# One stage for a layer's three attentions, and a row maximum ahead of the coefficients in attention B

## What is computed

```
s = einsum(q, k) * 64 ** -0.5;  p = softmax(s)
a = p[:, :, 0] - lam * p[:, :, 1]
o = einsum(a, v)
```

## Time and profile before

| | |
|---|---|
| median of 3 runs | 5782.29 us (5776.59 to 5786.37) |
| the profiled execution, its own time | 5787.31 us |
| its span | 5785.7 us |
| busy share: PE, PE weight loads, DVE, ACT, POOL | 84%, 72%, 53%, 45%, 20% |
| mean granted TensorE clock | 0.919 of full speed |
| the six attention stages, first PE instruction to last DVE output | 679 to 1012 (A), 1041 to 1295 (B), 1313 to 1493 (C); layer 1: A ends 3895, B 3923 to 4140, C 4157 to 4312 |

### The profile page before, as it was taken

One profiled execution on the slowest core, in us unless ns is written; L12 is line 12 of the kernel. 1 busy time (PEld: TensorE's weight loads), 2 busy tenths in 40 slices (PEclk: granted clock), 3 DMA queues, 4 the chain that ended last, 5 costly groups with the idle time before them and its releaser, 6 DMA issues. The chain is left out here.

```text
span 5785.7 us, 81996 instructions
## 1 busy us (share of the span) xinstructions
PE 4841.5 (84%) x28941; PEld 4176.1 (72%) x28941; DVE 3075.4 (53%) x4748; ACT 2589.9 (45%) x3394; POOL 1180.8 (20%) x1097
## 2 busy tenths in 40 slices
PE   5688899688798877799982788998889897599995
PEld 0688889678686776688762788987787686487774
DVE  1555155566433444677756551546563433577775
ACT  0344245456422331677762342545552221377773
POOL 0344200450000000333333340005300000233333
PEclk7799999899899988899996999998999998799997
DMA  8433441415333354799986432224353325599997
GB/s 370 168 94 96 180 146 39 100 50 125 127 120 135 139 204 169 285 397 397 397 324 226 152 95 85 62 50 109 76 142 117 144 106 190 192 397 397 397 397 288
DMA packets 596310, 1111.39 MB, mean 192 GB/s; under 512 B 112400, under 2 KB 295984, under 8 KB 589456
## 3 DMA queue, kind: packets, MB, share of 16 engines
q1 hardware_dynamic: 550576, 956.42, 48.1%
q0 software_dynamic: 29504, 94.50, 4.2%
q10 hardware_dynamic: 16032, 57.88, 2.5%
HBM read 908.23 MB, written 200.45 MB: 192 GB/s over the span
## 5 line engine op out<-in xcount | busy, mean ns | idle before, releaser
L643 PE MATMUL project_proj_acc<-project_w_split,project_hT 128*128 128x256 f32 x5472 | 727.7, 293 | 0.0
L643 PEld LDWEIGHTS project_proj_acc<-project_w_split,project_hT 128*128 128x128 f32 x5472 | 697.1, 200 | 0.3 <-issue 0.2
L1455 PE MATMUL merge_acc<-merge_hT,merge_w_split 128*128 128x512 f32 (+1 forms) x2880 | 634.1, 376 | 20.6 <-issue 16.9
L1455 PEld LDWEIGHTS merge_acc<-merge_hT,merge_w_split 128*128 128x128 f32 x2880 | 508.3, 191 | 129.6 <-issue 22.1
L2062 DVE TENSOR_TENSOR experts_w_gate<-experts_raw_gate,experts_w_gate 128x2048 fp32r<-128x2048 f32 x148 | 368.7, 2498 | 362.2 <-ACT experts_w_gate L2014 362.1
L1999 POOL TENSOR_TENSOR experts_w_down<-experts_raw_down,experts_w_down 128x2048 fp32r<-128x2048 f32 x74 | 361.4, 4883 | 536.9 <-ACT experts_w_down L2014 536.9
L2109 PE MATMUL experts_gate_acc<-experts_w_gate,experts_rowsT 128*128 128x512 f32 x1776 | 437.3, 402 | 13.8 <-DVE experts_rowsT L2067 10.1
L2123 PE MATMUL experts_result_acc<-experts_w_down,experts_hiddenT 128*128 128x512 f32 x1776 | 436.5, 401 | 12.2 <-DVE experts_w_down L2062 12.2
L2109 PE MATMUL experts_up_acc<-experts_w_up,experts_rowsT 128*128 128x512 f32 x1776 | 426.4, 395 | 0.0
L2109 PEld LDWEIGHTS experts_gate_acc<-experts_w_gate,experts_rowsT 128*128 128x128 f32 x1776 | 332.3, 190 | 101.6 <-issue 18.4
L2014 ACT CAST experts_w_gate<-experts_raw_gate 128x2048 fp32r<-128x2048 f32 x148 | 282.4, 1913 | 269.3 <-DMA experts_raw_gate<-in_w_exp_gate_dram 197.5
(11 more groups left out here) (220 smaller groups left out, 8506.6 us busy)
## 6 DMA issues: line engine op xcount, KB each, us to landing
experts_raw_gate<-in_w_exp_gate_dram SPq DMA_DIRECT2D x148, 1024.0 KB, 13.9
experts_raw_up<-in_w_exp_up_dram SPq DMA_DIRECT2D x148, 1024.0 KB, 12.9
experts_raw_down<-in_w_exp_down_dram SPq DMA_DIRECT2D x148, 1024.0 KB
merge_w_raw<-in_w_merge_dram SPq DMA_DIRECT2D x120, 768.0 KB, 6.6
modulation_w_ada<-in_w_ada_dram SPq DMA_DIRECT2D x48, 1024.0 KB, 27.1
qk<-project_staged SPq DMA_DIRECT2D x168, 256.0 KB, 2.3
ye<-experts_result ACTq DMA_DIRECT2D x74, 512.0 KB, 6.3
ye<-attend_a_zeros POOLq DMA_DIRECT2D x52, 512.0 KB, 27.4
```

Of the source, the lines that this page charges most:

```text
L643: m = pe.matmul(acc[s % 4][:, 0:HALF], hT[:, a, k, t * P:(t + 1) * P], w_split[hf][:, c, k, :], start=(i == 0 and k == 0), stop=(i == 2 an ...
L1455: m = pe.matmul(acc[:, bank, 0:w], w_split[b][:, a, k0 + k, :], act_T[:, x, kk, 0:w], start=(i == 0 and k == 0), stop=(i == 2 and k == n - 1))
```

## The change

Four edits:

1. The three attention stages become one, stage_attend. stage_attend_gqa and stage_attend_b turn into functions that return their parts per engine. Each engine runs A's, B's and C's part one after another, without a barrier between. A and C share their SBUF buffers, all three share the unit matrix and the PSUM buffers. B has its own SBUF buffers. SP issues A's first loads, then B's first loads (the four lambda vectors, head 0, and head 1 without its queries), then A's loop, then C's first loads, B's loop, C's loop, and then waits for all outputs. C's first loads wait for A's last scores and values. PE starts B when A's last output is ready (A's yd), and C when B's is.
2. In B, DVE takes the row maximum of set 0 of step s ahead of the coefficients of step s-1.
3. In project, the first table alone is made before POOL's loop, and needs only the rotary table and the first gain. The other five are made in group 0, one after each of POOL's steps 2 to 6. DVE waits for 3 table instructions in front of its first L555, and for all 18 at the end of group 0.
4. In output_and_route, the second activation tile is loaded between the w_out rows (after k = 5), the unit matrix and router weights come before the modulation rows, and PE waits for them after the products of tile 1 instead of after those of tile 0.

```diff
@@ project_heads
             for n, kind in enumerate(KINDS):
-                sp.dma_start(gain[:, n, :], io[kind][l].partition_broadcast(P)).then_inc(tab_in.sem, 16)
+                sp.dma_start(gain[:, n, :], io[kind][l].partition_broadcast(P)
+                             ).then_inc((more_in if n else tab_in).sem, 16)
...
                     if isinstance(g, int) and g == 0:
-                        dve.wait_ge(tab.sem, tab.done(6 * 3 - 1))
+                        dve.wait_ge(tab.sem, tab.done(3 - 1))
...
+                if isinstance(p, int) and p == 0:
+                    dve.wait_ge(tab.sem, tab.done(6 * 3 - 1))
...
                     if exists(q):
                         rest_of_heads(q, r)
+                    if isinstance(p, int) and p == 0 and s in range(2, 2 + 5):
+                        if s == 2:
+                            pool.wait_ge(more_in.sem, more_in.done(4))
+                        make_table(s - 1)
+                if isinstance(p, int) and p == 0:
+                    pool.wait_ge(tab.sem, tab.done(6 * 3 - 1))
+            pool.wait_ge(tab_in.sem, tab_in.done(1))
+            make_table(0)
+            pool.wait_ge(tab.sem, tab.done(3 - 1))
             pairs(pool, body)
@@ attend_gqa, SP: the first load of C
+            if isinstance(i, int) and i == 0 and first:
+                sp.wait_ge(first.qk.sem, first.qk.done(4 * NS - 1))
+                sp.wait_ge(first.pv.sem, first.pv.done(4 * NS - 1))
@@ attend_gqa, PE
+        if banded:
+            pe.wait_ge(const_split.sem, const_split.done(1))
+            pe.wait_ge(before_it.yd.sem, before_it.yd.done(before_it.last))
+        else:
+            pe.wait_ge(const_in.sem, const_in.done(0))
@@ attend_b, SP
+    def sync_first(sp):
+        load_kv, load_q, _ = loads(sp)
+        y_out.credit(sp)
+        for j, name in enumerate(("lambda_q1", "lambda_q2", "lambda_k1", "lambda_k2")):
+            sp.dma_start(lam_in[:, j, :], io[name][l].partition_broadcast(P)).then_inc(lam_ld.sem, 16)
+        load_kv(0, 0, None)
+        load_q(0, 0)
+        load_q(0, 1)
+        load_kv(1, 1, None)
@@ attend_b, DVE
             for s in range(nq):
+                row_max(n, s, 0)
                 q, r = before(n, s - 1)
                 if exists(q):
                     coefficients(q, r)
-                row_max(n, s, 0)
                 row_max(n, s, 1)
@@ stage_attend
+                sp.dma_start(shared.ident[:, :], io["k_ident"]).then_inc(shared.const_in.sem, 16)
+                a.sync_first(sp)
+                b.sync_first(sp)
+                a.sync(sp)
+                c.sync_first(sp)
+                b.sync(sp)
+                c.sync(sp)
+                for part in (a, b, c):
+                    part.sync_last(sp)
...
+            def _(pe):
+                for part in (a, b, c):
+                    part.tensor(pe)
@@ output_and_route, SP
                 sp.dma_start(w_raw[k % RAW][:, :], io["w_out"][l, k * P:(k + 1) * P, :]).then_inc(w_in[k % RAW].sem, 16)
-                if k == 1:
-                    load(0, 0)
+                if k in (1, 5):
+                    load(0, k // 5)
+            sp.dma_start(ident[:, :], io["k_ident"]).then_inc(const_in.sem, 16)
+            sp.dma_start(wr[:, :, :], io["w_router"][l]).then_inc(const_in.sem, 16)
             mod_rows(scr, l, 2, gate[:, :, :], sp).then_inc(rows_in.sem, 16)
             mod_rows(scr, l, 3, shift[:, :, :], sp).then_inc(rows_in.sem, 16)
             mod_rows(scr, l, 4, scale[:, :, :], sp).then_inc(rows_in.sem, 16)
-            load(0, 1)
-            sp.dma_start(ident[:, :], io["k_ident"]).then_inc(const_in.sem, 16)
-            sp.dma_start(wr[:, :, :], io["w_router"][l]).then_inc(const_in.sem, 16)
@@ output_and_route, PE
                         first_output()
-                        pe.wait_ge(const_in.sem, const_in.done(1))
                     else:
                         output(p, b)
+                    if isinstance(t, int) and t == 1:
+                        pe.wait_ge(const_in.sem, const_in.done(1))
```

More of the change, by code:

```diff
@@ new lines, in attend_gqa, with by_dve, wait_copied, before @@
+    steps = [Step(s % nq, banded) for s in range(NS)]
+    n_dve = sum(sx.n > sx.by_act for sx in steps)
+    def by_dve(i, s):
+        if steps[s].n > steps[s].by_act:
+            return i * n_dve + sum(sx.n > sx.by_act for sx in steps[:s])
+    def wait_copied(eng, i, s):
+        if exists(i):
+            eng.wait_ge(ca.sem, ca.done(i * NS + s))
+            if by_dve(i, s) is not None:
+                eng.wait_ge(cv.sem, cv.done(by_dve(i, s)))
+    def before(i, s):
+        return (i, s) if s >= 0 else (i - 1, s + NS)
@@ new lines, in attend_b, with before @@
+    lm, cf, df, tr, ca, pv, rc, yd = (
+        st.event("lambda_step"), st.event("coefficient_step"), st.event("b_difference"),
+        st.event("b_probs_transposed"), st.event("b_copied_out"), st.event("b_values_summed"),
+        st.event("b_reciprocal"), st.event("b_out_ready"))
+    dd, p1_scaled = st.event("difference_by_dve"), st.event("p1_scaled")
+    taken = st.event("pool_waits_taken")
+    steps = [Step(t, False) for t in range(nq)]
+    def before(n, s):
+        return (n, s) if s >= 0 else (n - 1, s + nq)
@@ new lines, in sync_first, with sync @@
+    def sync_first(sp):
+        load_kv, load_q, _ = loads(sp)
[6 more added lines that the diff above has]
+        load_kv(1, 1, None)
+    def sync(sp):
+        load_kv, load_q, store = loads(sp)
+        load_q(1, 0)
+        load_q(1, 1)
+        store(0)
+        with sp.Fori(2, NH) as n:
+            load_kv(n, n % 2, n - 2)
+            load_q(n, 0)
+            load_q(n, 1)
+            store(n - 1)
+        store(NH - 1)
@@ L1086, in score @@
-                def score(n, s, c):
-                    sx = steps[s]
-                    for col, a, w in sx.runs:
-                        for half in range(2):
-                            k = keys[:, ds(n % 2, 1), c, half, a * P:(a + w) * P].rearrange("p o n -> p (o n)")
-                            m = pe.matmul(scores[(s + c) % 2][:, col:col + w * P], queries[:, c, sx.t * P:(sx.t + 1) * P], k,
-                                          start=(half == 0), stop=(half == 1))
-                    m.then_inc(qk[c].sem, 1)
```

893 lines of the change are left out of this document (435 added, 458 removed).

## The result

| | before | after |
|---|---|---|
| median | 5783.19 us (5776.59 to 5786.37, 4 runs) | 5923.99 us (5923.15 to 5926.87, 4 runs) |
| ratio | | 1.0246, 95% interval 1.0228 to 1.0264 |
| span of the profiled execution, mean clock | 5785.7 us, 0.919 | 5925.3 us, 0.910 |

What follows compares the result with a forecast made beforehand. PE, busy 84% of the span, loses time at attention borders and in B's ring with other engines. Gains of -106 and losses of +211 gave +105 us: median 5888 us, own range about 5860 to 5915, 8 in 10 5825 to 5960.

Steps and rivals of the forecast that it cites:

- B's order: In B, the maximum moved ahead of the previous step's coefficients costs 2.65 us in each of 59 steps, 156 us.
- The ring: In B: scores, maximum, coefficients, POOL, transposes, next scores wait on each other in turn; 8.97 us per step against 6.32.
- The clock: In B's longer steps PE idles and its clock partly falls: 0.8 us per step taken, 47 us over 59 steps.
- The mixed steps: In B, the 11 mixed steps lose less than heavy ones: 8 us taken, between 0 and 29.
- The borders: Between attention stages, PE's idle 92.6 us shrink to 2.8, so 89.8 us go.
- The clears: Semaphore clears are not saved but moved to the end of C: 2 us per layer, 4 (0 to 10).
- The warm starts: At the attention borders PE starts warm, first scores run faster: 1.5 us per start, 6 us gained (0 to 10).
- A's loads: On SP, A's next loads stand behind B's early ones but are needed only after 20 steps, so loads are covered.
- The rival with a queue that holds A's loads back: B's early loads queue ahead of A's, or C's come late; half the border gain lost: +45, 5933 us, chance 0.07.
- The tables: In project, DVE's wait of 21.9 us goes but 17 us of delays beside tables come: 5 us gained (22 to 0).
- The contention: In project, DVE instructions beside POOL's table instructions run longer, 1.10 us each; 11 to 22 us, 17 taken.
- The output's start: In output_and_route, tile 0's transposes start earlier, at 2154.5 instead of 2159.8: 4.5 us per layer, 9 gained (0 to 22).

Runs made afterwards that it cites:

- run 1: Changed kernel with only the order in B undone (coefficients of the step in front before the maximum of set 0 again): 5682.5 us, ratio 0.9822.
- run 2: Kernel before with only the new order in B (maximum of set 0 ahead of the previous step's coefficients): 6020.1 us, ratio 1.0411.
- run 4: Changed kernel with B's difference split at six tenths: DVE takes 768 of 1280 columns, POOL 512: 5895.2 us, ratio 1.0191.
- run 5: Changed kernel, but in B DVE takes the previous step's coefficients, then the maximum of set 0, then the left difference: 5780.3 us, ratio 0.9999.
- run 3: Changed kernel plus 16 unused unit-matrix transposes on PE in front of each heavy B step's transposes: 5853.1 us, ratio 1.0116.
- run 7: run 6 with five of the six rotary tables left out, all heads using the first (computes something else): 5657.9 us, ratio 0.9787.
- run 9: run 6 with the five tables' 15 instructions spread over group 0, each behind the norm DVE makes ahead: 5658.0 us, ratio 0.9781.
- run 6: run 1 with B's first 24 loads issued behind A's last load and last store but one, instead of ahead of A's loop: 5666.6 us, ratio 0.9803.

## Why the prediction was right

**B's order.** The ring that the prediction described is there, term by term. The prediction had 1.47 + 1.59 + 0.68 + 4.14 + 1.09 = 8.97 us; the step at full clock took 1.44 from scores to maximum, 2.28 from there to POOL, 4.21 to the transposes and 1.07 to the scores, 9.00 in all. Against the mean step of 6.40 before, 59 steps give 153 us; forecast were 156. One detail was wrong: DVE idles for 4.10 us in front of the first maximum, not 1.4, because it runs out of work long before the transposes end. Runs 1 and 2 show that nothing else made the loss, and runs 4 and 5 that the ring runs through POOL: a cheaper POOL part shortens it, and POOL released ahead of the wait opens it.

**The clock.** This term was mis-sized: 47 us forecast, 71 measured (run 3). The two prices of a step that is low in both parts were nearly right. The transposes take 2.39 us instead of 1.31, so that the next scores start after 2.04 us instead of 1.07, and scores to maximum take 2.52 instead of 1.44. What failed is the share of the low time, 30% from the 0.85 in project, which the prediction raised by judgement from 0.65 to 0.8 us per step. The kernel after loses 1.23 us per step (10.23 - 9.00). In B the mean clock is 0.83, nearly that of project, but the low time lies just behind the idle stretch: of 30 steps in layer 1, 24 have all their transposes low, 6 of these the whole way from scores to maximum as well, and the other 18 a part of it (1.74 to 1.94 us). A mean over a stretch says little about the instructions behind its gaps. The rule of the Trainium skill (TensorE: Matmul & The Clock Gate, Why this matters for your kernels) names only longer gaps than most of these as a danger to the clock, and by it this term is 0. Here a gap of 2.3 to 3.2 us came in every heavy step of layer 1 behind the first, and filling the gaps was worth 71 us, so the measurement decides against it.

**The mixed steps.** 8 us were forecast. In layer 0 a head takes about 2 us more than its seven heavy steps account for, some 9 in all, the clock included.

**The borders.** -89.8 forecast, -90.0 measured. **The clears** cost 3.0 per layer, 6.0 instead of 4. **The warm starts** were to give 6. B's first scores take 2.59 instead of 4.61 us, twice. C of layer 1 is 2.1 shorter. But C of layer 0 is 3.7 us longer. The clock in its first 27.5 us was 0.69, and 0.83 before; in run 1 it was 0.94, and this stage was 5.7 us shorter than in the kernel after. Run 7 had 0.69 there too, behind a B at full clock, so this loss is not shown to be edit 2's. The stretch in the kernel after:

```profile
1394.80:1422.30 27.50, 26.24 (x152) 25.33 (x153) 13.54 (x45) 13.12 (x35) 0.00 (x0) 0.69 0.08 25
```

**A's loads.** Here the prediction failed in a sentence: A's next loads stand behind B's and "are needed only after 20 steps". They were needed at 758.75, 84 us behind A's start, and came at 774.99. The sentence counted the loads by the 28.45 us that they took at the border; beside POOL's zeros SP took 61 us to issue them, until 739.1, and 21.52 us more for the store behind. In layer 1, without the zeros, the same loads took 28 us. The rival with a queue that holds A's loads back named this place and priced it at 45 us over both layers; it was 16, in layer 0 alone.

**The tables.** -5 forecast, -8.6 measured. The wait of 21.9 us is gone as said. The contention was put at 17; four steps that are 1.45 us longer and one that is 0.58 longer make 6.4 per layer, 12.8, and 21.9 - 12.8 = 9.1. L511 was not near 2.3 but at 1.7; it was L508 that took 2.26. By the other rule cited, that of the Trainium skill (GPSIMD Engine Reference, Specifications), the edit would have brought nothing; the contention exists, as it says, but costs less than the wait that it replaces.

**The output's start.** -9 forecast, -16.9 measured for the whole experts stage. Tile 0's transposes begin 7.3 us earlier in layer 0 (41.9 us behind the first load instead of 49.2), where 4.5 were taken:

```profile
2224.63 11.41 PE L1734 MATMUL experts_out_acc<-experts_w_out,experts_mT 128*128 128x512 f32 x48
...
2227.87 1.23 DVE L1705 TENSOR_SCALAR experts_scale_rows<-experts_scale_rows 128x2048 f32<-128x2048 f32 x1 [7.26 <-DMA experts_scale_rows<-mod]
...
2237.66 1.06 PE L1744 MATMUL experts_hT_acc<-experts_ident,experts_h_tile 128*128 128x128 f32 x8 [1.62 <-DVE experts_h_tile L1697]
```

The scale rows came 32.1 us behind the first load instead of 30.3, not 4 us later, so DVE's norm was ready sooner than the working had it.

**The sum.** In the spans the change cost 139.6 us, 35 more than forecast. B cost 31 more (237.8 against 211 less the 4 that its warm starts give), A's late load 14, C's start 4, the clears 2. Tables and output gave 12 more than forecast, and merge, which the change does not touch, was 4 shorter; in layer 0 it lies between 608.5 and 612.8 us over the eleven profiles, so this is scatter. That the total came within 36 us is thus in part luck: what tables and output gave beyond the forecast hid about a quarter of what B, A's loads, C's start and the clears cost beyond it.

## What to carry to other kernels

On an engine that works in order, an instruction that waits for this step's result must not stand ahead of those that finish the last step: everything behind it inherits the wait, and if one of these instructions releases the engine that is waited for, a ring closes. Before moving such an instruction, write down the ring that results and compare it with the step; here five rows gave 8.97 us against 6.32, and the chip 9.00. Merging stages is worth its borders only if the loads that are moved ahead don't stand in front of loads that are due sooner. The gain of 101 us and the loss of 237 were in one change, so parts with different mechanisms are best timed apart.

## What the runs showed of the hardware

- Of two large instructions of DVE and POOL on SBUF data, the one that starts second is longer, as if it waited for the first: DVE's 128x640 took 1.76 us instead of 0.89 behind POOL's, POOL's 128x640 took 2.46 instead of 1.89 behind DVE's. Even DVE's 128x1024 with one tensor input took 1.32 us instead of 0.69 beside a table in layer 0, though 0.72 beside one in layer 1. Tables spread out and kept apart from DVE's two large instructions, with no work less, shortened project by 14 us (run 9 against run 6).
- 16 useless transposes in each heavy step of B made the changed kernel 71 us faster: the granted clock in a stretch of B was 1.00 instead of 0.83.
- SP took 21.52 us to issue one store in layer 0, beside B's loads and POOL's zeros, and 0.39 us for the same one in layer 1, without the zeros. What stood behind it in SP's queue went out that much later.
